# A recurrent scan wholly in 64x64 products, its transposed inverse carried through the solve, its jobs in two pairs of PSUM banks

## The chip, the cores and the metric

The kernel runs on one NeuronCore of a Trainium2 chip. The metric is the device time of one execution in microseconds. Its engines are TensorE (matrix products, PE in the rows, with the loading of weights as PEld), VectorE (DVE), ScalarE (ACT), GpSimd (POOL) and SyncE (SP, which issues the transfers here). Matrix products write to PSUM, eight banks of 2 KB in each of 128 partitions; VectorE and ScalarE copy them out.

## The reference, cut to what matters

The reference is a network of three blocks on 512 tokens of width 1024 with 256 context tokens. The second block has a recurrent scan over 16 heads of width 64, in two directions:

```python
def step(S, inp):
    w_t, k_t, v_t, kk_t, kka_t = inp[:5]
    S = (S * w_t[:, :, None, :]
         - jnp.einsum('bhij,bhj->bhi', S, kk_t)[..., None] * kka_t[:, :, None, :]
         + v_t[..., None] * k_t[:, :, None, :])
    y = jnp.einsum('bhij,bhj->bhi', S, inp[5]) if emit else None
    return S, y
```

S is a 64x64 state for each head and direction. After the scan the outputs are normalised for each head, scaled, added to a bonus term and gated. The rest (attention, pooling, the feed-forward layers, the projections) isn't touched by the change.

## The kernel before

The function `wkv` computes the scan. It takes the tokens in chunks of 64 (`CHUNK`), 12 for the 768 tokens, and replaces the steps within a chunk by matrix products and by the inverse of a triangular 64x64 matrix; only the states between chunks are passed on one after another. The heads go in eight pairs, one pair a phase `k` of `phases()`; while pair k is solved, pair k+1 is prepared and pair k-1 is finished. Three parts of the order matter.

The first is the list of *jobs* that `solve_jobs` writes out. Each job is a batch of small products into PSUM, which one engine then copies out. A pair's 12 chunks in two directions and two heads are 48 matrices, worked on in three groups g of 16. For each group M, N and I multiply the prepared keys with each other (copied by ScalarE or VectorE); K multiplies with the values. Then the inverse is built from small blocks up, in five levels (`LEVELS` is 2, 4, 8, 16, 32), three groups each, so 15 solves (`SOLVES`): Z multiplies the matrix M by the present inverse x, and VectorE keeps the part that the level adds by a predicated copy with a mask (line 2783); X multiplies that by the present inverse transposed, which gives the next inverse, and ScalarE copies it (line 2657). For X the transposed inverse is needed: U makes it by four 128x128 transposes through the identity into bank 7 (line 2445), copied by ScalarE (line 2661), anew at every level. At the last level T takes the place of X and gives the transposed inverse itself (line 2470). E, P, B and Y apply the inverse to keys and values and form what the states and the outputs need.

The second is the ring of banks. Jobs lie in banks 0 to 3, two banks wide (K's first two one), in the order of the list; a job waits until whatever lay in its banks has been copied out (`ring_free`). In the solve this gives Z one pair of banks and X the other. U has bank 7, and waits for the copy of the U before. Banks 4 and 5 serve the preparation (two alternating single banks), and bank 6 the steps from state to state and the outputs.

The third is what is woven between the jobs (`woven_stages`). After the jobs M, N, I stand the scan steps of pair k-1 (`step`, ten, 8 matmul records each) and the turns of tokens (`tok`): 14 stages of three 128x128 transposes, each copied by ScalarE. Around K and the first Z stand the low-rank products (`lora`, eight stages of one 64x128 product with 384 columns) and `ystate`; along the solve stand the sums of squares (`sums`, `yvar`), which multiply 128x128 blocks with two columns of a mask, and the spreads (`spread`, `yspread`), which hand one value back to 64 columns. Each engine runs this list in its own order; no scheduler changes it. SyncE only loads each pair's inputs and stores its result.

A 64x64 product is addressed to one of four quarters of the array, by the half of the partitions that its inputs lie in and the half that its output goes to. Z, X, M, N and I rotate over all four; K and E use only the two where rows and columns are the same half, since their output partitions are those of the input (`ps[f, ...]`).

## Time and profile before

| | us |
|---|---|
| median of three runs | 3102.48 |
| lowest and highest | 3100.88, 3104.81 |
| span of the profiled execution (slowest and only core) | 3107.0 |
| TensorE busy | 2828.0 (91%) |
| VectorE busy | 1827.1 (59%) |
| ScalarE busy | 1219.8 (39%) |

The profile gives no other time for its execution than the span, from its first to its last instruction. TensorE's busy time counts matmuls whose ends are modelled and overlap, so four products on four quarters count once; a full row doesn't mean an engine at its peak. The scan stands between about 1228 and 1900 us of the span. In the rows, `residual` and `work` are memory that the scan borrows: `residual` holds M and the inverse x (and, in the listing of the changed kernel, both inverses), `work` the tokens, the starting inverse and its transpose.

### The profile page before, as it was taken

The numbers are of one execution on the slowest core, as the hardware profiler recorded it, in microseconds if no ns is written. First come the engines' busy times: TensorE is split into PE (matmuls) and PEld (weight loads), VectorE is DVE, ScalarE is ACT, GpSimd is POOL, SyncE is SP. The second block draws the span as 40 slices with busy tenths as digits, with TensorE's granted clock in tenths as the row PEclk, the third lists the DMA queues.
The fourth block names the chain that finished last, engine by engine and source line by source line (L and its number), as shares of the span: only waits on it lengthen the run. The fifth ranks groups of instructions, "written<-read, shape, count | busy, mean of one in ns | idle before, by whom it ended". The sixth has DMA issues, their size and how long they took to land. (4 is left out here: it accounts for less than half of the span.)

```text
span 3107.0 us, 66043 instructions
## 1 busy us (share of the span) xinstructions
PE 2828.0 (91%) x28892; PEld 2454.0 (79%) x28892; DVE 1827.1 (59%) x2841; ACT 1219.8 (39%) x2024; POOL 18.9 (1%) x25
## 2 busy tenths in 40 slices
PE   4988989999997998898899988899998898889998
PEld 4977989999996887677777776688886685678887
DVE  7656775655446644666666655755567644466642
ACT  4326343222224433555555543433334324454421
POOL 0011000000000000000000000000000000000000
PEclk9999989999996999999999998899998898999999
DMA  6320223333321323100000003355531210123332
GB/s 256 121 87 23 89 94 124 127 138 126 122 80 57 114 96 128 32 24 10 25 26 26 26 13 112 120 181 178 176 111 57 61 42 8 55 75 96 101 94 83
DMA packets 89981, 272.88 MB, mean 88 GB/s; under 512 B 9441, under 2 KB 14689, under 8 KB 89569
## 3 DMA queue, kind: packets, MB, share of 16 engines
q1 hardware_dynamic: 85088, 258.17, 24.4%
q10 hardware_dynamic: 4608, 10.49, 1.0%
q8 instruction: 231, 3.78, 0.5%
q14 instruction: 54, 0.43, 0.0%
HBM read 252.11 MB, written 16.52 MB: 86 GB/s over the span
## 5 line engine op out<-in xcount | busy, mean ns | idle before, releaser
L427 DVE TENSOR_TENSOR weights_low<-raw_weights,weights_high 128x1024 fp32r<-128x1024 f32 (+3 forms) x333 | 356.5, 1072 | 704.5 <-ACT weights_high L396 703.8
L396 ACT ACTIVATE weights_high<-raw_weights 128x1024 fp32r<-128x1024 f32 (+3 forms) x333 | 310.9, 935 | 975.1 <-PE psum L223 934.2
L223 PE MATMUL psum<-mlp_in_high,weights_high 128*128 128x512 f32 (+1 forms) x1120 | 371.4, 368 | 21.5 <-DVE mlp_in_low L964 16.4
L223 PE MATMUL psum<-mlp_in_low,weights_high 128*128 128x512 f32 (+1 forms) x1120 | 369.9, 367 | 0.0
L223 PE MATMUL psum<-mlp_in_high,weights_low 128*128 128x512 f32 (+1 forms) x1120 | 369.7, 367 | 0.0
L223 PEld LDWEIGHTS psum<-mlp_in_high,weights_high 128*128 128x128 f32 x1120 | 208.7, 190 | 49.3 <-issue 17.6
L223 PE MATMUL psum<-hidden_high,weights_high 128*128 128x384 f32 (+1 forms) x768 | 229.5, 352 | 0.0
L223 PE MATMUL psum<-hidden_low,weights_high 128*128 128x384 f32 (+1 forms) x768 | 229.5, 352 | 0.0
L223 PE MATMUL psum<-hidden_high,weights_low 128*128 128x384 f32 (+1 forms) x768 | 229.4, 352 | 0.0
L223 PEld LDWEIGHTS psum<-mlp_in_low,weights_high 128*128 128x128 f32 x1120 | 209.1, 190 | 24.2
L223 PEld LDWEIGHTS psum<-mlp_in_high,weights_low 128*128 128x128 f32 x1120 | 208.8, 190 | 24.3
L2783 DVE COPY_PREDICATED wkv_z<-wkv_levels,psum 128x512 f32<-128x512 int32 x120 | 87.9, 733 | 103.6 <-PE psum L2466 101.9
L223 PEld LDWEIGHTS psum<-hidden_high,weights_low 128*128 128x128 f32 x768 | 140.5, 188 | 10.1
L223 PEld LDWEIGHTS psum<-hidden_low,weights_high 128*128 128x128 f32 x768 | 140.5, 188 | 10.0
L223 PEld LDWEIGHTS psum<-hidden_high,weights_high 128*128 128x128 f32 x768 | 140.5, 188 | 9.9
L223 PE MATMUL psum<-mixed_high,weights_high 128*128 128x384 f32 (+1 forms) x360 | 108.5, 366 | 25.4 <-DVE mixed_low L1309 11.9
L223 PE MATMUL psum<-h_high,weights_high 128*128 128x384 f32 (+2 forms) x312 | 100.7, 372 | 23.4 <-DVE h_low L964 20.2
L223 PE MATMUL psum<-mixed_low,weights_high 128*128 128x384 f32 (+1 forms) x360 | 105.6, 358 | 0.0
L223 PE MATMUL psum<-mixed_high,weights_low 128*128 128x384 f32 (+1 forms) x360 | 105.4, 358 | 0.0
L699 DVE CUSTOM_DVE_ANT_0 pool_u<-pool_u,conditions 128x1024 f32<-128x1024 f32 x80 | 97.6, 1220 | 0.8
L223 PE MATMUL psum<-h_high,weights_low 128*128 128x384 f32 (+2 forms) x312 | 97.6, 363 | 0.0
L223 PE MATMUL psum<-h_low,weights_high 128*128 128x384 f32 (+2 forms) x312 | 97.5, 362 | 0.0
(477 smaller groups left out, 5581.2 us busy)
## 6 DMA issues: line engine op xcount, KB each, us to landing
raw_weights<-in_mlp_w SPq DMA_DIRECT2D x96, 512.0 KB, 4.3
mod_space<-in_ada SPq DMA_DIRECT2D x56, 512.0 KB, 3.7
pool_u<-in_ada SPq DMA_DIRECT2D x56, 512.0 KB, 3.6
raw_weights<-in_w_up SPq DMA_DIRECT2D x44, 512.0 KB, 3.5
work<-in_ada SPq DMA_DIRECT2D x32, 512.0 KB, 4.8
raw_weights<-in_mlp_w SPq DMA_DIRECT2D x64, 256.0 KB, 2.9
raw_weights<-in_w_down SPq DMA_DIRECT2D x16, 512.0 KB, 3.5
raw_weights<-in_w_in SPq DMA_DIRECT2D x12, 512.0 KB, 4.8
```

Of the source, the lines that this page charges most:

```text
L223: last = nc.tensor.matmul(out[:, a, :] if wide else out, w[:, cols], x[:, at, t0:t1], start=first, stop=final)
L396: nc.scalar.activation(halves_of(ph, j)[0], raw_of(ph, j), ACT.Copy).then_inc(high.sem, 1)
L427: nc.vector.tensor_tensor(lo, raw_of(ph, j), hi.bitcast(F32), ALU.subtract).then_inc(split.sem, 1)
L699: ins = nc.vector.tensor_tensor_reduce(out=self.junk, in0=self.w[:, slot, :], in1=vector, scale=1.0, scalar=0.0, op0=ALU.mult, op1=ALU.add ...
L2783: last = nc.vector.copy_predicated(two(Z[:, i // GROUPS, i % GROUPS % 2, :]), level(2 + i // GROUPS), ps[:, b:b + 2, 0:4 * CHUNK])
```

## The change

The transposed inverse is no longer made anew at each level by transposes. U remains for the three starting inverses, as 16 products of 64x64 with a 64x64 identity; after that T, which multiplies the old transposed inverse by the masked product, runs at every level and not only at the last, 15 jobs in place of 3. Z's result is laid out so that T's and X's outputs fall in the partitions that the next level wants, and the masks follow this. All jobs of the list, U too, take a pair of banks, and all share two pairs, (0,1) and (2,3), in turn (`ring_slots`); bank 7 holds the bonus. K and E write to all four quarters.

In the woven stages every product is 64x64 in its weights: seven turns of tokens with 24 products each in place of 14 with three transposes, which now use banks 4 and 5 together; four lora stages of four products in place of eight of one; sums, variances, mean, spreads and bonus are split likewise. Sums, mean, variances and the outputs' spread move from bank 6 to banks 4 and 5. The two operations of VectorE that read a spread are cut along the half banks. The core of the diff:

```diff
-        jobs += [("M", g, 2, "SV" if g else "S"), ("N", g, 2, "V"), ("I", g, 2, "V")]
-    jobs += [("K", 0, 1, "S"), ("K", 1, 1, "S"), ("K", 2, 2, "S")]
-    for i in range(SOLVES + 2):
+        jobs += [("M", g, "SV" if g else "S"), ("N", g, "V"), ("I", g, "V")]
+    jobs += [("K", g, "S") for g in range(GROUPS)]
+    for i in range(SOLVES + 1):
         if i < SOLVES:
-            jobs.append(("Z", i, 2, "V"))
+            jobs.append(("Z", i, "V"))
         if i < GROUPS:
-            jobs.append(("U", i, 0, "S"))
-        if 1 <= i <= SOLVES:
-            jobs.append(("X" if i - 1 < SOLVES - GROUPS else "T", i - 1, 2, "S"))
-        if 2 <= i and i - 2 < SOLVES - GROUPS:
-            jobs.append(("U", i - 2 + GROUPS, 0, "S"))
-    jobs += [("E", g, 2, "S") for g in range(GROUPS)]
+            jobs.append(("U", i, "S"))
+        if i >= 1:
+            if i - 1 < SOLVES - GROUPS:
+                jobs.append(("X", i - 1, "S"))
+            jobs.append(("T", i - 1, "S"))
+    jobs += [("E", g, "S") for g in range(GROUPS)]
     for g in range(GROUPS):
-        jobs += [("P", g, 2, "V"), ("B", g, 2, "V")]
-    return jobs + [("Y", 0, 2, "V")]
+        jobs += [("P", g, "V"), ("B", g, "V")]
+    return jobs + [("Y", 0, "V")]
...
+def ring_slots(jobs):
+    used = {0: -2, 2: -1}
+    held, place, earlier = {}, {}, {}
+    for at, (name, i, _) in enumerate(jobs):
+        b = min((0, 2), key=lambda b: used[b])
+        place[name, i], earlier[name, i] = b, (held.get(b), False)
+        held[b], used[b] = (name, i), at
+    for job, (before, _) in earlier.items():
+        if before is None:
+            earlier[job] = held[place[job]], True
+    return place, earlier
...
-    at = {("M", 0): [("tok", 0), ("tok", 1), ("step", 1)], ("N", 0): [("tok", 2), ("tok", 3), ("step", 2)],
...
+    at = {("M", 0): [("tok", 0), ("step", 1)], ("N", 0): [("tok", 1), ("step", 2)],
...
+                def ring_free(k, name, i):
+
+                    job, again = earlier[name, i]
+                    if k or not again:
+                        pe.wait_ge(*(by_vector if job in kept_v else by_scalar)(k - again, *job))
+                    if again and place[name, i] == 6:
+                        pe.wait_ge(*prep_kept(k, 3))
+                        if k >= 1:
+                            pe.wait_ge(y_kept.sem, y_kept.base + k)
...
-                                        f = rows_of(o)
-                                        n = (d * 2 + j) * 2 + h
-                                        weights = XT[f, i, h * 4 * CHUNK:(h + 1) * 4 * CHUNK][:, by_tile_order(d, j)]
-                                        last = nc.tensor.matmul(ps[f, b, n * CHUNK:(n + 1) * CHUNK], weights,
+                                        f, to, n = rows_of(o), rows_of(j), d * 2 + h
+                                        weights = XX[f, i, 1, h * 4 * CHUNK:(h + 1) * 4 * CHUNK][:, by_tile_order(d, j)]
+                                        last = nc.tensor.matmul(ps[to, b + o, n * CHUNK:(n + 1) * CHUNK], weights,
                                                                 TOK[f, 2, own(tile_of(d, 2 * i + j), h)], start=True, stop=True)
...
+                                        f, to, c = rows_of(o), rows_of(d), (h * 2 + j) * CHUNK
+                                        last = nc.tensor.matmul(ps[to, b + o, c:c + CHUNK], X1[f, i, unit(h, d, j)], EYE[f, :],
+                                                                start=True, stop=True)
...
-                            last = nc.tensor.transpose(ps[:, 7, c], x[:, c], core.ident[:, :])
...
+                                        f, to, c = rows_of(o), rows_of(side), (h * 2 + same) * CHUNK
+                                        last = nc.tensor.matmul(ps[to, b + o, c:c + CHUNK], AA[f, g, unit(h, d, j)],
+                                                                x[f, x_columns(level - 1, h, d, j)], start=True, stop=True)
...
+                                        f, to, c = rows_of(side), rows_of(o), (h * 2 + same) * CHUNK
+                                        last = nc.tensor.matmul(ps[to, b + side, c:c + CHUNK], XX[f, g, 1, t_columns(level - 1, h, d, j, o)],
+                                                                Z[f, level, g % 2, z_columns(level, h, d, j, o)], start=True, stop=True)
...
+                                        side, over = row_side(level, d, j), row_side(level + 1, d, j)
+                                        f, to, c = rows_of(side), rows_of(over), (h * 2 + o) * CHUNK
+                                        last = nc.tensor.matmul(ps[to, b + side, c:c + CHUNK],
+                                                                Z[f, level, g % 2, z_columns(level, h, d, j, o)],
+                                                                XX[f, g, 1, t_columns(level - 1, h, d, j, o)], start=True, stop=True)
...
-                                        f, u = rows_of(o), unit(h, d, j)
-                                        n = (d * 2 + j) * P
-                                        last = nc.tensor.matmul(ps[f, b + h, n:n + P], XT[f, i, u],
-                                                                RHS[f, d, (2 * i + j) * 2 + h, :, :].rearrange("p s c -> p (s c)"),
+                                        f, to, n = rows_of(j), rows_of(o), (h * 2 + d) * P
+                                        last = nc.tensor.matmul(ps[to, b + j, n:n + P], XX[f, i, 1, t_columns(len(LEVELS) - 1, h, d, j, o)],
+                                                                RHS[f, i, o, d * 2 + h, :, :].rearrange("p s c -> p (s c)"),
                                                                 start=True, stop=True)
...
-                        for j in range(3):
-                            t = n % 2 * 3 + j
-                            if n // 2 in (1, 2, 3, 4):
-
-                                t = tile_of((n // 2 - 1) % 2, t)
-                            last = nc.tensor.transpose(ps[:, prep_bank(k, TURN + n), j * P:(j + 1) * P],
-                                                       src[:, t * P:(t + 1) * P], core.ident[:, :])
...
+                        for p in range(tiles):
+                            t = tile_of((n - 1) % 2, p) if 1 <= n <= 4 else p
+                            for o in range(2):
+                                for h in range(2):
+                                    f, to = rows_of(h), rows_of(p % 2 if 1 <= n <= 2 else o)
+                                    c = (p // 2 * 2 + o if 1 <= n <= 2 else p) * CHUNK
+                                    last = nc.tensor.matmul(ps[to, 4 + h, c:c + CHUNK], src[f, at_chunk(t, o)], EYE[f, :],
+                                                            start=True, stop=True)
...
-                        nc.tensor.matmul(ps[:, prep_bank(k, BONUS), :], core.head_sum[:, :], BON[:, :], start=True, stop=True)\
-                            .then_inc(prep_done.sem, 1)
...
+                        for h in range(2):
+                            f = rows_of(h)
+                            last = nc.tensor.matmul(ps[f, 7, :], core.ones[f, 0:HEAD], BON[f, :], start=True, stop=True)
...
-                                last = nc.tensor.matmul(ps[rows_of(h), prep_bank(q, SPREAD + n), j * P:(j + 1) * P],
-                                                        small[:, 0, 1, 2 * t + h:2 * t + h + 1].to_broadcast([P, HEAD]),
-                                                        core.ident[:, :], start=True, stop=True)
...
+                                    last = nc.tensor.matmul(ps[rows_of(h), 4 + o, t * CHUNK:(t + 1) * CHUNK],
+                                                            small[f, 0, 1, c:c + 1].to_broadcast([HEAD, HEAD]), EYE[f, :],
+                                                            start=True, stop=True)
...
-                    elif name == "T":
-                        last = act(by_tile(XT[:, i % GROUPS, :]), filled(b), ACT.Copy)
-                    elif name == "U":
-                        last = act(XT[:, i % GROUPS, :].rearrange("p (o m c) -> p m o c", o=2, c=CHUNK),
-                                   ps[:, 7, :].rearrange("p (m o c) -> p m o c", o=2, c=CHUNK), ACT.Copy)
+                        last = act(two(XX[:, i % GROUPS, 0, :]), half_pair(name, i), ACT.Copy)
+                    elif name in "TU":
+                        last = act(two(XX[:, i % GROUPS, 1, :]), half_pair(name, i), ACT.Copy)
                     else:
-                        for h in range(2):
-                            last = act(MX[:, i, h * 512:(h + 1) * 512], ps[:, b + h, :], ACT.Copy)
+                        last = act(two(MX[:, i, :]), ps[:, b:b + 2, :], ACT.Copy)
```

In the solve, TensorE's list reads as follows before, around the spreads of `X6` (L2466 is Z, L2468 X, L2445 U, L2585 and L2630 the two spreads):

```order
L2468 MATMUL psum<-wkv_z,work 64x64 x16
L2585 MATMUL psum<-constants,wkv_small 64x128 x12
L2630 MATMUL psum<-constants,wkv_small 64x128 x8
L2445 MATMUL psum<-constants,residual 128x128 x4
L2466 MATMUL psum<-residual 64x64 x16
```

And in the changed kernel at the same place (L2481 is Z, L2493 X, L2506 T, L2637 the first spread; the second now stands two solves later):

```order
L2481 MATMUL psum<-residual,work 64x64 x16
L2493 MATMUL psum<-wkv_z,residual 64x64 x16
L2637 MATMUL psum<-wkv_eye,wkv_small 64x64 x24
L2506 MATMUL psum<-residual,wkv_z 64x64 x16
L2481 MATMUL psum<-residual,work 64x64 x16
```

Four transposes of 128x128 between X and Z have become 16 products of 64x64. Each f32 product of this kind leaves two matmul records in a trace, each transpose one.

At the start of a pair, TensorE before (L2409 M and N of group 0, L2418 I, L2407 M and N of later groups, L2554 the turns, L2602 the scan steps):

```order
L2409 MATMUL psum<-wkv_exc_rho,wkv_a 64x64 x16
L2554 MATMUL psum<-constants,wkv_v 128x128 x6
L2602 MATMUL psum<-wkv_b,wkv_t 64x64 x4
L2409 MATMUL psum<-wkv_exc_rho,wkv_kd 64x64 x16
L2554 MATMUL psum<-constants,wkv_exc_rho 128x128 x6
L2602 MATMUL psum<-wkv_s,wkv_t 64x64 x4
L2418 MATMUL psum<-wkv_a,wkv_exc_rho 64x64 x16
L2554 MATMUL psum<-constants,wkv_exc_rho 128x128 x3
```

And in the changed kernel (L2436, L2445, L2434 are the same jobs, L2595 the turns, L2654 the steps):

```order
L2436 MATMUL psum<-wkv_exc_rho,wkv_a 64x64 x16
L2595 MATMUL psum<-wkv_eye,wkv_v 64x64 x24
L2654 MATMUL psum<-wkv_b,wkv_t 64x64 x4
L2436 MATMUL psum<-wkv_exc_rho,wkv_kd 64x64 x16
L2595 MATMUL psum<-wkv_eye,wkv_exc_rho 64x64 x24
L2654 MATMUL psum<-wkv_s,wkv_t 64x64 x4
L2445 MATMUL psum<-wkv_a,wkv_exc_rho 64x64 x16
L2595 MATMUL psum<-wkv_eye,wkv_exc_rho 64x64 x24
```

The places of jobs, turns and steps stay; a turn of three or six transposes has become one of 24 products.

## Rows read from the trace of the kernel before

**Rows 1.** The page: span, and TensorE's matmul row of part 1.

```profile
span 3107.0 us, 66043 instructions
PE 2828.0 (91%) x28892; PEld 2454.0 (79%) x28892; DVE 1827.1 (59%) x2841; ACT 1219.8 (39%) x2024; POOL 18.9 (1%) x25
```

**Rows 2.** Windows of one pair: sections A, B and C; columns in the first line.

```profile
core 0: us, PE busy (x) PEld busy (x) DVE busy (x) ACT busy (x) POOL busy (x), PEclk, DMA share, GB/s
1325.48:1350.47 24.99, 24.72 (x584) 19.21 (x584) 16.36 (x37) 13.93 (x30) 0.00 (x0) 1.00 0.07 19
1350.47:1388.47 38.00, 34.00 (x1089) 27.87 (x1088) 24.80 (x39) 24.51 (x45) 0.00 (x0) 1.00 0.01 3
1388.47:1405.77 17.30, 13.40 (x472) 12.21 (x463) 10.07 (x19) 3.85 (x7) 0.00 (x0) 1.00 0.27 80
```

**Rows 3.** Timeline of a solve: start, duration, engine, line, operation, count [idle before].

```profile
1375.18 0.69 PE L2466 MATMUL psum<-residual 64*64 64x64 f32 x32
1375.69 0.66 PE L2468 MATMUL psum<-wkv_z,work 64*64 64x64 f32 x32
1375.94 0.73 DVE L2783 COPY_PREDICATED wkv_z<-wkv_levels,psum 128x512 f32<-128x512 int32 x1
...
1376.28 0.66 PE L2445 MATMUL psum<-constants,residual 128*128 128x128 f32 x4
1376.40 0.60 ACT L2657 ACTIVATE residual<-psum 128x512 f32<-128x512 f32 x1 [0.53 <-PE psum L2468]
...
1376.86 0.69 PE L2466 MATMUL psum<-residual 64*64 64x64 f32 x32
```

**Rows 4.** Timeline of TensorE between two gaps marked issue, later in the solve.

```profile
1378.48 0.46 PE L2468 MATMUL psum<-wkv_z,work 64*64 64x64 f32 x16 [0.69 <-issue]
1378.88 0.66 PE L2445 MATMUL psum<-constants,residual 128*128 128x128 f32 x4
1379.46 0.69 PE L2466 MATMUL psum<-residual 64*64 64x64 f32 x32
1379.98 0.65 PE L2468 MATMUL psum<-wkv_z,work 64*64 64x64 f32 x32
1380.56 0.66 PE L2445 MATMUL psum<-constants,residual 128*128 128x128 f32 x4
1381.14 0.69 PE L2466 MATMUL psum<-residual 64*64 64x64 f32 x32
1381.65 0.29 PE L2468 MATMUL psum<-wkv_z,work 64*64 64x64 f32 x4
1382.50 0.68 PE L2468 MATMUL psum<-wkv_z,work 64*64 64x64 f32 x28 [0.55 <-issue]
```

**Rows 5.** Timeline of TensorE: three pairs of neighbouring gaps, least, median and greatest distance.

```profile
1400.85 0.45 PE L2498 MATMUL psum<-wkv_a_ga,residual 64*64 64x128 f32 x8 [0.80 <-issue]
...
1404.32 0.27 PE L2533 MATMUL psum<-wkv_gk,work 64*64 64x64 f32 x1 [0.23 <-issue]
...
1780.19 0.45 PE L2466 MATMUL psum<-residual 64*64 64x64 f32 x13 [0.20 <-issue]
...
1784.12 0.62 PE L2466 MATMUL psum<-residual 64*64 64x64 f32 x25 [0.42 <-issue]
...
1464.00 0.27 PE L2466 MATMUL psum<-residual 64*64 64x64 f32 x1 [0.86 <-issue]
...
1468.82 0.45 PE L2466 MATMUL psum<-residual 64*64 64x64 f32 x13 [1.13 <-issue]
```

**Rows 6.** The page, part 3, DMA queues: packets, MB, share of 16 engines' span.

```profile
q8 instruction: 231, 3.78, 0.5%
```

**Rows 7.** Timeline of TensorE: the bonus product, two K jobs, and the E jobs.

```profile
1340.29 1.12 PE L2560 MATMUL psum<-wkv_bonus,constants 128*128 128x512 f32 x2
...
1345.80 2.03 PE L2430 MATMUL psum<-work 64*64 64x64 f32 x64
...
1388.47 5.42 PE L2481 MATMUL psum<-residual,work 64*64 64x128 f32 x91
```

**Rows 8.** A window at the start of the first pair, columns as in group 2.

```profile
1249.00:1250.40 1.40, 1.15 (x33) 1.03 (x34) 1.36 (x3) 0.00 (x0) 0.00 (x0) 0.50 0.00 0
```

More of the change, by code:

```diff
@@ L2134, in wkv @@
     jobs = solve_jobs()
-    positions, at = [], 0
-    kept_s, kept_v, place = {}, {}, {}
+    place, earlier = ring_slots(jobs)
+    kept_s, kept_v = {}, {}
     n_s = n_v = 0
-    for name, i, width, keeper in jobs:
+    for name, i, keeper in jobs:
         if "S" in keeper:
@@ L2572, in stage @@
+                        for h in range(2):
+                            for d in range(2):
+                                f, c = rows_of(d), which * P + h * HEAD
+                                last = nc.tensor.matmul(ps[rows_of(h), b + d, 0:T0 // 2], ups[f, c:c + HEAD],
+                                                        (lora_w, lora_a)[which][f, a * T0 // 2:(a + 1) * T0 // 2], start=True, stop=True)
+                        last.then_inc(prep_done.sem, 1)
                     elif name == "sums":
@@ L2617, in stage @@
                         pe.wait_ge(y_kept.sem, y_kept.base + k)
-                        nc.tensor.matmul(ps[:, 6, :], core.head_mean[:, :], Y0[:, :], start=True, stop=True)\
-                            .then_inc(mean.sem, 1)
+                        if k < DT:
+                            pe.wait_ge(*(lora_kept(q, LORAS) if q < DT else turn_kept(k, 6)))
+                        for h in range(2):
+                            f = rows_of(h)
+                            last = nc.tensor.matmul(ps[f, 4, :], core.head_mean[f, f], Y0[f, :], start=True, stop=True)
+                        last.then_inc(mean.sem, 1)
                     elif name == "yvar":
@@ L2727, in _ @@
                 for k in phases():
[L2728 removed]
+                    for name, i, keeper in jobs:
                         if 0 <= k < DT and "S" in keeper:
@@ L3629, in wkv_masks @@
     both = [(level(1).T, level(1)), (level(1), level(1).T)]
[L3630 removed]
+    inverse = [(level(n), level(n).T) for n in LEVELS[1::2]]
+    sided = [level(n) for n in LEVELS[0::2]]
     last = [(i < j, i > j), (i <= j, i >= j)]
[L3632 to L3635 removed]
+    across = [np.concatenate((d0, d1, d0, d1), axis=1) for d0, d1 in inverse]
+    out = [np.concatenate((d0, d0, d1, d1), axis=1) for d0, d1 in both + last]
+    out = [np.concatenate([m, m], axis=0) for m in out[:len(both)]] + \
+        [np.concatenate([np.tile(sided[n // 2], 4), np.tile(sided[n // 2].T, 4)], axis=0) if n % 2 == 0
+         else np.concatenate([across[n // 2], across[n // 2]], axis=0) for n in range(len(LEVELS))] + \
+        [np.concatenate([m, m], axis=0) for m in out[len(both):]]
+    return np.stack(out, axis=1).astype(np.float32)
 def lay_out(i):
```

357 lines of the change are left out of this document (182 added, 175 removed).

## The prediction

> **What bounds the kernel now.** I read the page first, for the span and for the number of TensorE instructions [rows 1]; then the lines by tile, to find the stage that the change touches; then its windows [rows 2]; then the timeline of that stage, first for one undisturbed iteration of the solve [rows 3], then for the places where TensorE waits for nothing that the profile shows [rows 4, 5].
>
> The span is 3107.0 us [rows 1]; outside the scan nothing changes. A pair of heads costs about 80.3 us, in three sections [rows 2]: A (M, N, I, K, the turns of tokens, the scan steps) 24.99 us with 584 matmul records, B (the solve: Z, U, X, T) 38.00 us with some 1086, C (E, P, B, Y) 17.30 us with 472 in the window, 456 by the program. There are eight pairs, some 640 us together; the first lacks the scan steps, the last the preparation of a next pair.
>
> In B an undisturbed iteration takes 1.68 us: Z starts at 1375.18, X 0.51 later, U 0.59 after that, the next Z 0.58 after U [rows 3]. Thirty-two records of a 64x64 job are issued in 0.51 us, 16 ns each. But 15 iterations of 1.68 are 25 us, not 38. Part of the rest is woven work; part is gaps marked "issue". These gaps recur with a strange regularity. From 1378.48 to 1382.50 there are 16+4+32+32+4+32+4 = 124 matmul records and then 0.55 us of nothing [rows 4]. Each record has its weight load, so that is 248 instructions, and with the waits between them about 256. The page has a queue of kind "instruction" with 231 packets and 3.78 MB, 16.4 KB each [rows 6]; 2 x 28,892 TensorE instructions [rows 1] over 231 packets is 250 a packet. So a gap stands where TensorE has used up one packet of its program and the next has not come. Over the eight pairs I find 15 neighbouring gaps that are 123 to 127 records apart; their distances go from 3.47 us (1400.85 to 1404.32) over a median of 3.93 (1780.19 to 1784.12) to 4.82 (1464.00 to 1468.82) [rows 5]. A block of some 124.5 records seems not to come faster than once in 3.9 us, whatever is in it. Section B before uses 8.7 blocks in 38.0 us, 4.4 us each: it is already near that limit.
>
> The page "Runtime: NRT & Kernel Launch" of the Trainium skill, section "Instruction fetch mechanics", also has blocks of 256 instructions fetched while the current one runs, and says that crossing a block costs little and is mostly hidden, because instructions are consumed more slowly than they are fetched. The size agrees with the 124 records; the hiding does not, with gaps of 0.55 and 1.13 us [rows 4, 5].
>
> **The change part by part.** What it does to the number of TensorE records per pair is what I cost first. A 64x64 product in f32 is two records (32 for 16 products), a transpose through the 128x128 identity is one (4 for 4) [rows 3].
> - U: 15 jobs of 4 go (-60), 3 jobs of 32 come (+96). T: 3 jobs of 32 become 15 (+384).
> - In B also: key sums 12 to 48, variances 8 to 32, the two spreads 24 to 48 and 16 to 32, mean 2 to 4, the last lora 4 to 8: +36 +24 +24 +16 +2 +4. B goes from 1086 to 1612 records.
> - In A: 14 turns of 3 transposes (42) become 7 of 24 products (336), lora 12 to 24, bonus 2 to 4: 584 becomes 892. C keeps 456.
>
> The sum is 2960 against 2126, 23.8 blocks against 17.1.
>
> Section B. 1612/124.5 = 12.95 blocks. One is ready when the section begins, and I let it run at its own pace, 2.6 us; the others come at 3.93: 11.95 x 3.93 + 2.6 = 49.6 us, against 38.00: +11.6. By 3.64 a block it would be 46.1, by 4.4 it would be 55.2.
>
> Beneath that cover lies the ring. Before, Z and X each had a pair of banks and U bank 7; now Z, X and T share two pairs, and each job waits until the one two before it is copied out. X to its copy's end is 0.71 + 0.60 us (1375.69, 1376.40), Z's 0.76 + 0.73 (1375.18, 1375.94) [rows 3]; with 0.15 to restart TensorE (my choice, from copies that a U followed) these are 1.46 and 1.64. Three jobs over two pairs of banks: (1.64 + 1.46 + 1.46)/2 = 2.28 us an iteration, against 1.68. But 96 records at 124.5 in 3.93 us are 3.03 us an iteration. So the ring's wait costs nothing as long as instructions come this slowly; without that cover it is +0.6 an iteration.
>
> Section A. Up to the bonus there are 688 records, 5.5 blocks: 4.5 x 3.93 + 2.6 = 20.4 us, against 14.8 before (1325.48 to 1340.29 [rows 2, 7]). Behind it come K, lora and the states' product, 204 records; large products, 10.2 us before, which the stream doesn't hold up. K loses something: its 64 records take 2.03 us, 32 ns each, as they use two quarters of the array, and now use four at 16 ns [rows 7]; 96 records save 1.5 us of TensorE, of which I take 0.7, because the lora copies on ScalarE are one behind another there. 9.5 us. A: 29.9, +4.9.
>
> Section C. E's first 91 records take 5.42 us, 60 ns each, on two quarters [rows 7]. On four, about 30 ns, a job takes 0.95 us, and the copies of twice 512 columns (2 x 0.60 at most, by X's copy [rows 3]) decide: the second E is copied 0.95 + 0.25 + 2.4 = 3.6 us after the first began, and P, which takes its banks, starts there instead of 5.2 us behind. I take -1.8. C has 3.7 blocks, 14.4 us at 3.93, below the 15.5 left, so the saving stands, with little to spare.
>
> All else I cost at nothing: ScalarE copies as many solve jobs as before, half as many turns at twice the width; VectorE's work is the same but for operations cut in two. The turns hold banks 4 and 5 together now, so each waits for the copy of the one before, some 0.9 us for 768 columns by X's 0.60 for 512; an M, N or I job and a scan step lie between two turns, 0.65 to 1.1 us of TensorE, so it is 0 to 0.3 us each, 0 to 2 a pair. I take 0, since it lies beneath the stream's wait. ScalarE is busy 24.5 of B's 38 us and VectorE 24.8 [rows 2]. Spreads and sums take less of TensorE as 64x64 products (48 records at 16 ns are 0.8 us), but that time is given back to waiting for the next block.
>
> Per pair: +11.6 +4.9 -1.8 = +14.7 us. The first pair has 2748 records, the last 2832; I count the eight as 7.8 full ones: +115 us. Against its own span that is 3222. The span stands 4.5 us above the median of 3102.48 of the runs, so I predict 3217.
>
> "TensorEngine Tiling (Array Packing)" of the Trainium skill, section "Key Properties", says that a change of tiling mode drains TensorE. By it this change gains, since all modes but 64x64 leave the scan. The trace shows X to U 0.59 and Z to X 0.51 us apart [rows 3], 0.08 us a change. Some 60 changes a pair would be 5 us, and by that alone the sum would be 3063.
>
> **The rivals.**
> 1. Faster: the instruction stream isn't what limits. If the gaps were something else (a record lost, a semaphore), the mode changes, K, E and the cheaper spreads and sums would show. A gives back 1.8 us; B pays 0.6 x 6 for the ring in its undisturbed iterations and gives back 4.8 (my estimate: spreads 1.3, sums 1.0, mode changes 1.0, gaps 1.5); C gives back 1.8. That is -4.8 a pair, 3065 us. It decides at one point: A+B+C, by the sums above, is 16.5 L + 30.2, and this is 80.3 where L, the time of a block, is 3.04 us. All 15 measured are above (the least 3.47 [rows 5]). For it speaks only that records at 16 ns and no gap would allow 2.0 us a block. The Trainium skill's two rules above, fetching that is hidden and a mode change that drains, would both lead here.
> 2. Slower, but by the ring: blocks come in some 3.0 us when asked for early, and the two pairs of banks set 2.28 us an iteration: +8.9 in B less 4.8 for A, C and the spreads, +4 a pair, 3135 us. Against it stand the 3.03 us an iteration by [rows 5].
> 3. The clock falls too. In B 96 records of 16 ns in 3.0 us leave TensorE half idle. At the lower level (granted 0.50, 1.2 GHz) 33 records were busy 1.15 us [rows 8], against 0.69 for 32 at the full level. Before, all three sections ran at 1.00 [rows 2] with a gap of 1.1 us in the middle. Three jobs would then take 3.0 us an iteration, as long as the stream, and every wait would be 0.45 longer: some +4 a pair more, 3250 us.
>
> **How the numbers follow.** Forecast (the stream of instructions sets the pace) 0.75; rival 1 0.07; rival 2 0.10; rival 3 0.08. The forecast's own range is 3.64 to 4.2 us a block, 3180 to 3250. To leave out no more than 2 in 10 I go from 3135, which takes in rival 2, to 3270. What can be told from no change is 0.2%, 6 us. Slower: 0.75 + 0.10 + 0.08 = 0.93, less 0.03 for a rival 2 that comes out even: 0.90. Within 0.2%: 0.03. Faster: 0.07.
>
> **What would show it.** The packets of the instruction queue rise from 231 to about 283 (6550 more records in eight pairs, 13,100 instructions). B's window grows to about 50 us with TensorE's busy share falling, gaps marked "issue" at nearly every 124th record, 3.6 to 4.2 us apart, and few in C. The first E to P shrinks from 5.2 to about 3.5 us. VectorE's wait for Z grows though Z is no longer. Wrong would be: gaps further apart than 4.8 us or none while B still grows (then the ring, with TensorE waiting for ScalarE's copies of X and T), a granted clock below 0.95 in B, or a pair under 80 us.

## The result, and the profile after

The changed kernel takes 3197.72 us (3185.94 to 3200.68, four runs) against 3103.64 of the kernel before on the same chip: ratio 1.0291, 95% interval 1.0269 to 1.0314. That is 94 us more by the medians and 90 by the ratio; 115 were forecast, and 3217 us. The page after answers to [rows 1] and [rows 6]:

```profile
span 3193.2 us, 78968 instructions
PE 2787.4 (87%) x35564; PEld 2433.5 (76%) x35564; DVE 1826.9 (57%) x2849; ACT 1215.5 (38%) x1928; POOL 18.9 (1%) x25
...
q8 instruction: 282, 4.62, 0.6%
```

TensorE has 6672 matmul records more (eight times 834) and is busy 41 us less, in a span that is 86 us longer: it waits more. VectorE and ScalarE do the same work as before. The instruction queue brought 282 packets in place of 231.

The windows of pair 1, answering to [rows 2], sections A, B and C:

```profile
1332.26:1360.73 28.47, 22.73 (x893) 18.80 (x896) 14.47 (x35) 13.38 (x21) 0.00 (x0) 1.00 0.07 18
1360.73:1409.38 48.65, 33.81 (x1617) 28.87 (x1613) 26.54 (x42) 24.86 (x45) 0.00 (x0) 0.96 0.02 4
1409.38:1426.13 16.75, 11.53 (x471) 9.80 (x462) 10.22 (x19) 3.56 (x4) 0.00 (x0) 1.00 0.26 84
```

The means over pairs 1 to 6, which I use from here on, are 25.13, 38.16 and 17.06 us before and 28.82, 47.35 and 15.38 after: +3.7, +9.2, -1.7, together +11.2 us a pair. Times 7.8 that is 87 us, and the span grew by 86.2. In B TensorE's work is as long as it was for half as many records again, and TensorE's busy share falls from 90% (34.45 of 38.16) to 73% (34.51 of 47.35).

The timeline of TensorE late in a solve, for [rows 3] to [rows 5] (L2481 is Z, L2493 X, L2506 T, L2518 E):

```profile
1676.33 0.62 PE L2481 MATMUL psum<-residual,work 64*64 64x64 f32 x27 [0.48 <-issue]
...
1677.83 0.69 PE L2506 MATMUL psum<-residual,wkv_z 64*64 64x64 f32 x32 [0.35 <-DVE wkv_z L2842]
1678.35 0.65 PE L2481 MATMUL psum<-residual,work 64*64 64x64 f32 x32
1679.24 0.33 PE L2493 MATMUL psum<-wkv_z,residual 64*64 64x64 f32 x3 [0.25 <-ACT residual L2721]
1679.94 0.63 PE L2493 MATMUL psum<-wkv_z,residual 64*64 64x64 f32 x27 [0.37 <-issue]
...
1683.57 0.63 PE L2481 MATMUL psum<-residual,work 64*64 64x64 f32 x28 [0.37 <-issue]
...
1687.18 2.48 PE L2518 MATMUL psum<-residual 64*64 64x128 f32 x65 [0.47 <-issue]
```

Four gaps stand 3.61, 3.63 and 3.61 us apart, and between the last two there are 28+1+3+31+32+31 = 126 records by the rows left out. Over the eight pairs there are some 108 gaps of at least 0.15 us marked issue, 76.8 us in all, against 33 and 18.3 us before; over 70 of them follow the one before by one block, at a median of 3.65 us. Between the gaps waits for VectorE and ScalarE stand, and by the marks they are the larger part: in B a pair's waits for ScalarE's copies are 6.2 us (1.7 before), those marked issue 4.5 (1.5 before), those for VectorE 1.8 (0.5 before). So the marks alone don't say whether the stream or the ring of banks sets the pace; the experiments do.

The traces also hold the packets of the instruction queue one by one, each 16,384 bytes. Every gap marked issue in the scan, 33 before and over 100 after, ends 1.20 to 1.60 us after such a packet has been moved; 1676.33 to 1687.18, for example, has packets that end at 1678.54, 1682.36 and 1685.66 us, and TensorE resumes at 1679.94, 1683.57 and 1687.18. Of the waits put down to ScalarE only 12 of 138 end that long after a packet, of those to VectorE 5 of 64. So a gap marked issue ends with the arrival of instructions.

K and E, for [rows 7] (L2456 is K, L2538 P), and the start of the first pair, for [rows 8]:

```profile
1357.81 0.64 PE L2456 MATMUL psum<-work,residual 64*64 64x64 f32 x32
...
1775.26 2.03 PE L2518 MATMUL psum<-residual 64*64 64x128 f32 x64
1777.48 1.10 PE L2518 MATMUL psum<-residual 64*64 64x128 f32 x32 [0.19 <-ACT residual L2723]
1778.44 0.59 PE L2538 MATMUL psum<-wkv_a_ga,residual 64*64 64x64 f32 x24
```

```profile
1246.69:1248.09 1.40, 1.40 (x52) 1.40 (x56) 1.36 (x3) 0.20 (x1) 0.00 (x0) 0.50 0.00 0
```

E to P takes 3.18 us here, where no gap falls into it, and 4.0 to 4.6 us in the pairs where one does; it was about 5.2. The first pair begins at the granted clock of 0.50 (1.2 GHz), as before.

### The profile page after: what moved, and what is told of

It is laid out like the page before. It is cut to its first block and busy times, and to the rows that moved or that the text cites. A ratio compares the mean times of both kernels' runs of the same rounds, so it can differ in the third digit from the quotient of the medians.

```text
span 3193.2 us, 78968 instructions
## 1 busy us (share of the span) xinstructions
PE 2787.4 (87%) x35564; PEld 2433.5 (76%) x35564; DVE 1826.9 (57%) x2849; ACT 1215.5 (38%) x1928; POOL 18.9 (1%) x25
## 5 line engine op out<-in xcount | busy, mean ns | idle before, releaser
L223 PEld LDWEIGHTS psum<-hidden_high,weights_high 128*128 128x128 f32 x768 | 140.5, 188 | 10.1
L2721 ACT ACTIVATE residual<-psum 128x512 f32<-128x512 f32 x144 | 85.6, 595 | 80.9 <-PE psum L2506 68.3
L2506 PE MATMUL psum<-residual,wkv_z 64*64 64x64 f32 x3840 | 95.3, 231 | 22.0 <-issue 11.5
L2493 PE MATMUL psum<-wkv_z,residual 64*64 64x64 f32 x3072 | 75.5, 233 | 39.0 <-ACT residual L2721 29.8
```

Source lines behind the costliest of these rows:

```text
L223: last = nc.tensor.matmul(out[:, a, :] if wide else out, w[:, cols], x[:, at, t0:t1], start=first, stop=final)
L2493: last = nc.tensor.matmul(ps[to, b + side, c:c + CHUNK], XX[f, g, 1, t_columns(level - 1, h, d, j, o)], Z[f, level, g % 2, z_columns(level ...
L2506: last = nc.tensor.matmul(ps[to, b + side, c:c + CHUNK], Z[f, level, g % 2, z_columns(level, h, d, j, o)], XX[f, g, 1, t_columns(level - 1 ...
L2721: last = act(two(XX[:, i % GROUPS, 1, :]), half_pair(name, i), ACT.Copy)
```

## The experiments

Ratios are to the kernel before, in runs on the same chip. The kernel before takes 3109.89 us beside the first four, so by its ratio the changed kernel would take about 3200 us there. Two theories were set against each other: the stream (a block of some 125 records comes no faster than once in 3.65 us) and the ring (three solve jobs wait for each other's copies in two pairs of banks); a third is the sheer work of TensorE.

**t_turned: T below the last level by transposes, still in the ring.** From the changed kernel:

```diff
-            jobs.append(("T", i - 1, "S"))
+            jobs.append(("X" if i - 1 < SOLVES - GROUPS else "T", i - 1, "S"))
+        if 2 <= i and i - 2 < SOLVES - GROUPS:
+            jobs.append(("T", i - 2, "S"))
...
+                            pe.wait_ge(*by_scalar(k, "X", i))
+                            for side in range(2):
+                                for h in range(2):
+                                    c = side * 256 + h * P
+                                    out = ps[:, b + side, h * P:(h + 1) * P]
+                                    last = nc.tensor.transpose(out, XX[:, g, 0, c:c + P], core.ident[:, :])
```

> In the changed kernel the transposed inverse of the levels below the last is made again by four 128x128 transposes of X's result, in the same ring of two pairs of banks; all else stays, 64x64 products included. That is 28 matmul records less in each of 12 jobs a pair, 1276 in place of 1612 in the solve. If the stream of instructions sets the pace (3.65 us a block of 125 records, the median of the changed kernel's profile), the solve falls from 47.6 to about 38.5 us a pair and the kernel to about 3125 us. If the ring of banks sets it, the solve stays: 3190 to 3200 us. If TensorE's own work sets it, 12 jobs at 0.59 us take the place of 12 at 0.51: 3195 to 3205 us.

Measured: 3158.33 us, ratio 1.0156 (1.0134 to 1.0178). B falls from 47.35 to 42.71 us, A and C rise by 0.5 and 0.7. The sign is the stream's, the size lies between the two: 42 us of the 75 came.

**tok_turned: five of the seven turns of tokens by transposes.**

```diff
+                            if not 1 <= n <= 2:
+                                a, m = (p % 2, p // 2) if n > 2 and n < 5 else (p // 3, p % 3)
+                                last = nc.tensor.transpose(ps[:, 4 + a, m * P:(m + 1) * P], src[:, t * P:(t + 1) * P], core.ident[:, :])
+                                continue
```

> In the changed kernel five of the seven turns of tokens are made by six 128x128 transposes each again, 210 records less in section A of a pair; the solve is untouched. Stream of instructions: A falls from 28.5 by up to 1.7 blocks, 6 us, less what the changes of tile mode give; I expect 4 us a pair, the kernel near 3165 us. If the drains at changes of mode were what counts, ten of them come back a pair at some 0.1 us each: 3198 to 3210 us.

Measured: 3185.37 us, ratio 1.0243 (1.0223 to 1.0263). A falls from 28.82 to 26.32 us, but B rises from 47.35 to 48.77. The 210 records fewer a pair are 1.7 blocks, 6.2 us, of which A gave 2.5 and B took 1.4 back. The sign is again the stream's, at under half the size.

**wide_z: Z streams its operand twice, 128 columns in place of 64, with the same instructions and copies.**

```diff
-                                        last = nc.tensor.matmul(ps[to, b + o, c:c + CHUNK], AA[f, g, unit(h, d, j)],
-                                                                x[f, x_columns(level - 1, h, d, j)], start=True, stop=True)
+                                        out = ps[to, b + o, :].rearrange("p (a l) -> p a l", a=2)[:, :, c:c + CHUNK]
+                                        last = nc.tensor.matmul(out, AA[f, g, unit(h, d, j)],
+                                                                x[f, x_columns(level - 1, h, d, j)].unsqueeze(1).to_broadcast([HEAD, 2, CHUNK]),
+                                                                start=True, stop=True)
```

> In the changed kernel every product of the Z jobs streams its operand twice, the second copy into the unused half of the bank: 128 columns in place of 64, the same number of instructions, copies and waits. By the M and N jobs this makes a Z job some 0.45 us longer on TensorE, 6.7 us a pair. Stream of instructions: that is hidden while the next block is awaited, under 1 us a pair, 3195 to 3205 us. TensorE's work: +54 us, 3250 us. Ring of banks: Z's copy comes 0.45 us later, half of it in each iteration, +3.4 us a pair, 3225 us.

Measured: 3211.4 us, ratio 1.0328 (1.0305 to 1.0351), some 11 us above the changed kernel: more than the 3205 that the stream allowed, less than the ring's 3225, and far from the 3250 of TensorE's work. Its B by six windows, first and sum (the changed kernel's sum is 284.12 with PE 207.08):

```profile
1364.86:1413.96 49.10, 38.66 (x1617) 33.77 (x1612) 26.39 (x42) 24.94 (x45) 0.00 (x0) 0.97 0.02 4
...
sum 294.84, PE 235.36 PEld 204.64 DVE 158.87 ACT 149.83 POOL 0.00; mean PE 39.23 PEld 34.11 DVE 26.48 ACT 24.97 POOL 0.00
```

TensorE is busy 4.7 us a pair more in B, by the columns 480 records of 16 ns, 7.7 us, and B is 1.8 us longer, where under 1 was expected by the stream and 3.4 by the ring. TensorE's work isn't what holds section B, but a longer Z isn't wholly hidden either.

**both_turned: both of the first two edits.** Its diff is theirs together.

> Both edits before this one together, the levels' transposes and the five turns of tokens by 128x128 transposes: 2414 records a pair in place of 2960 (2126 in the kernel before). Stream of instructions: the two gains add, 3125 and 3165 from 3198 give about 3090 us, at which the stream is no longer short everywhere and the ring's waits begin to show; I expect 3095 us. Ring: 3190 us or more.

Measured: 3130.78 us, ratio 1.0065 (1.0044 to 1.0087), 36 us above the 3095 expected by the stream and well below the ring's 3190. The gaps fall to 35 with 24.3 us, nearly as few as before, so most of the stream's pressure is gone; yet B stays at 42.49 us. Here the ring can be seen (L2493 X, L2481 Z, L2506 T; L2732 is ScalarE's copy of T, L2730 of X):

```profile
1703.40 0.69 PE L2481 MATMUL psum<-residual,work 64*64 64x64 f32 x32
1703.51 0.60 ACT L2732 ACTIVATE residual<-psum 128x512 f32<-128x512 f32 x1 [1.07 <-PE psum L2506]
1704.16 0.69 PE L2493 MATMUL psum<-wkv_z,residual 64*64 64x64 f32 x32
...
1704.95 0.66 PE L2506 MATMUL psum<-constants,residual 128*128 128x128 f32 x4
...
1705.57 0.69 PE L2481 MATMUL psum<-residual,work 64*64 64x64 f32 x32
```

X begins 0.76 us after Z though Z's 32 records are issued in 0.51: T's copy frees its banks at 1704.11. An iteration is 2.17 us, against 1.68 [rows 3]. Where ScalarE has something else before that copy, X waits longer:

```profile
1701.07 0.69 PE L2493 MATMUL psum<-wkv_z,residual 64*64 64x64 f32 x32 [1.04 <-ACT residual L2732]
```

**out_of_ring: both_turned with those transposes in bank 7, outside the ring; the bonus moves to bank 4.**

```diff
+        if name == "T" and i < SOLVES - GROUPS:
+            place[name, i], earlier[name, i] = 7, (held.get(7), False)
+            held[7] = (name, i)
+            continue
         b = min((0, 2), key=lambda b: used[b])
```

> This is the kernel with levels' transposes and turns by transposes (3130.78 us, 0.65% above the kernel before), with the transposes of the levels put back into bank 7, outside the ring of two bank pairs; the three first U and the last three T stay in the ring. TensorE issues the same records in the same order. If what is left in section B (42.5 us against 38.2 in the kernel before, with 35 gaps in place of 108) is the ring, where each Z waits for the copy of the X or T two jobs before, B falls to about 38.5 us and the time by 4 us x 7.8 = 31 us to about 3100 us, a ratio of 0.997. If it is the stream of instructions, nothing changes: 3130 us, ratio 1.0065. If it is work of TensorE (the spreads, sums and lora as many small products), nothing changes either, and B stays at 42.5 us with few waits for ScalarE or VectorE.

Measured: 3106.96 us, ratio 1.0009 (0.9998 to 1.0021). B falls by 3.4 us, from 42.49 to 39.07. Six windows of B in both_turned, and in out_of_ring, by their sums:

```profile
sum 254.96, PE 208.63 PEld 166.43 DVE 161.16 ACT 149.68 POOL 0.00; mean PE 34.77 PEld 27.74 DVE 26.86 ACT 24.95 POOL 0.00
```

```profile
sum 234.42, PE 192.86 PEld 160.04 DVE 161.28 ACT 146.90 POOL 0.00; mean PE 32.14 PEld 26.67 DVE 26.88 ACT 24.48 POOL 0.00
```

In B TensorE's waits for ScalarE go from 4.4 us a pair to 1.3, and gaps marked issue come back: 77 with 53.7 us in place of 35 with 24.3. An iteration without a gap is 1.67 us again:

```profile
1708.27 0.70 PE L2485 MATMUL psum<-residual,work 64*64 64x64 f32 x32
...
1709.94 0.70 PE L2485 MATMUL psum<-residual,work 64*64 64x64 f32 x32
```

So the ring is real, and behind it the stream is met once more. Its size is less sure than the 3.4 us: the granted clock differed. In both_turned three pairs ran B at 1.00 and took 40.84, 40.95 and 41.65 us, and one ran at 0.85 and took 45.51; in out_of_ring four ran at 1.00, at a mean of 39.18. By the pairs at 1.00 alone the ring is worth 2.0 us. The ratio gives 17 us, 2.2 a pair, the spans 24.7 (3131.5 and 3106.8); expected were 31. The waits that the profile marks don't fall in sum (6.5 and 6.9 us a pair); the gain stands in TensorE's busy time, which takes in the start of each wait, as 32 records are issued in 0.51 us and count as busy for 0.69.

**fewest: out_of_ring with low-rank products, sums, variances and spreads in 128 rows again.** Of its diff, the sums:

```diff
-                            for o in range(2):
-                                for h in range(2):
-                                    f = rows_of(h)
-                                    last = nc.tensor.matmul(ps[rows_of(o), 4 + h, t:t + 1], SQ[f, at_chunk(t, o)], core.ones[f, 0:1],
-                                                            start=True, stop=True)
+                            last = nc.tensor.matmul(ps[:, 4, t:t + tiles + 1:tiles], SQ[:, t * P:(t + 1) * P],
+                                                    core.head_sum[:, 0:P:HEAD], start=True, stop=True)
```

> The kernel of out_of_ring with the low-rank products, sums, variances and spreads again as products of 128 rows, some 116 records a pair fewer (2298 against 2414; the kernel before has 2126). What stays of the change: Z, X and E laid out for four quarters, the turns with three transposes each in banks 4 and 5, and K, P and E on four quarters. By the stream: 116 records are 0.93 blocks of 124.5; where blocks limit, 3.65 us a pair, but few gaps are left (24 us in all), so I expect 1 to 2 us a pair, 8 to 15 us: 3085 to 3092 us, ratio 0.992 to 0.995. By the ring as the only cause: the same as out_of_ring within 3 us. By the mode change: eight lora products a pair and the spreads of 64x128 change mode again, 0.08 us each, some 30 a pair, +2.4 us a pair: slower than out_of_ring by 10 to 20 us.

Measured: 3102.11 us, ratio 0.9985 (0.9976 to 0.9994). B falls to 37.5 us, but A rises from 25.8 to 26.4: a gain of 7 us by ratios, under the 8 to 15 expected (3085 to 3092 us). In section A it shows two waits, of which the kernel before has only the second, at 0.26 us in place of 0.38:

```profile
1507.46 0.38 PE L2666 MATMUL psum<-wkv_s,wkv_t 64*64 64x64 f32 x5 [1.04 <-DVE wkv_s L2960]
...
1508.76 0.92 PE L2629 MATMUL psum<-lora_input,wkv_ups 64*128 64x384 f32 x4 [0.38 <-DVE wkv_bonus_value L2886]
```

**leaner: fewest with a change against each of those two waits, the bonus in bank 7 and the low-rank stage ahead of the ninth step.**

```diff
-          ("I", 2): [("bonus", 0), ("step", 9)],
-          ("K", 0): [("lora", 0), ("step", 10)], ("K", 1): [("lora", 1), ("square", 0), ("decay", 0)],
+          ("I", 2): [("bonus", 0), ("lora", 0), ("step", 9)],
+          ("K", 0): [("step", 10)], ("K", 1): [("lora", 1), ("square", 0), ("decay", 0)],
...
-                            last = nc.tensor.matmul(ps[f, 4, :], core.ones[f, 0:HEAD], BON[f, :], start=True, stop=True)
+                            last = nc.tensor.matmul(ps[f, 7, :], core.ones[f, 0:HEAD], BON[f, :], start=True, stop=True)
```

> The kernel of fewest (3102.11 us, 0.15% under the kernel before), with its new waits in section A taken away: the bonus is back in bank 7 (the transposes of the levels, which have that bank since, are done by then), so the first low-rank stage no longer waits for VectorE to use the bonus (0.38 us idle in fewest's third pair), and that stage moves ahead of the ninth scan step, which waited 1.04 us for the state copied before it. The records are the same, 2298 a pair. In fewest section A is 26.4 us against 25.1 before, with 2.2 us a pair of waits for VectorE against 1.1. If these two waits are what A lost, A falls by 1.0 to 1.4 us a pair, 8 to 11 us in all: 3091 to 3095 us, ratio 0.995 to 0.996. If A is held by the stream or by the double-width turns of tokens, which wait for the copy of the one before: no change within 3 us.

Measured: 3083.11 us, ratio 0.9934 (0.9920 to 0.9948): it is faster than both kernels, and by more than the 0.995 to 0.996 expected. A falls by 1.27 us to 25.11, as the two waits said in sum, but not by them alone. The bonus's wait is gone; the state's 1.04 us is now 0.20 before the ninth step and 0.68 before the tenth; and a wait of 0.96 us of the next low-rank stage for ScalarE (decay) is gone too. B and C fall by 0.85 and 0.67, which was not expected. In part that is the choice of runs: the profile is of the fastest of leaner's five runs (3077.46 us), and fewest's is of the second slowest of twelve (3104.23). The spans differ by 26.8 us, the ratios by 16, and A's 1.27 us a pair is 10. Its B:

```profile
1347.31:1384.11 36.80, 34.13 (x1175) 28.53 (x1173) 26.09 (x40) 24.50 (x45) 0.00 (x0) 0.95 0.02 4
...
sum 220.02, PE 198.61 PEld 165.75 DVE 155.62 ACT 146.89 POOL 0.00; mean PE 33.10 PEld 27.63 DVE 25.94 ACT 24.48 POOL 0.00
```

**burst: the kernel before with 1024 independent products at the start of the scan.** Nobody reads what they write.

```diff
+                for n in range(1024):
+                    f, to = rows_of(n % 2), rows_of(n // 2 % 2)
+                    nc.tensor.matmul(ps[to, 6 + n % 2, 0:CHUNK], core.ident[f, 0:CHUNK], core.ident[f, 0:CHUNK],
+                                     start=True, stop=True)
```

> The kernel before with 1024 independent 64x64 products of the identity (2048 matmul records, 4096 instructions, 16.4 blocks) at the start of TensorE's program of the scan, into two banks that nothing else holds there, with no wait between them; their output is read by nobody. They measure the block period by itself. By the stream: the gaps stand 124 to 128 records apart, and a block takes 3.5 to 3.9 us whatever it holds: 16.4 x 3.65 = 60 us more, ratio 1.019; TensorE is busy 2.0 us of each 3.7. By work alone: 16 ns a record at the full clock, 33 us more, or up to 66 us at the lower granted clock with no gaps marked issue. If the period depends on waits and semaphores of the scan, not on the number of instructions: no gaps, 33 us.

Measured: 3166.45 us, ratio 1.0204 (1.0187 to 1.0221), 63 us. TensorE's timeline, the whole burst but for rows that repeat:

```profile
1227.06 3.95 PE L2637 MATMUL psum<-constants 64*64 64x64 f32 x252 [1.29 <-PEq L349]
1235.10 3.69 PE L2637 MATMUL psum<-constants 64*64 64x64 f32 x128 [4.09 <-issue]
1239.37 2.79 PE L2637 MATMUL psum<-constants 64*64 64x64 f32 x128 [0.58 <-issue]
1243.10 2.10 PE L2637 MATMUL psum<-constants 64*64 64x64 f32 x128 [0.94 <-issue]
1246.57 2.10 PE L2637 MATMUL psum<-constants 64*64 64x64 f32 x128 [1.37 <-issue]
1250.31 2.10 PE L2637 MATMUL psum<-constants 64*64 64x64 f32 x128 [1.65 <-issue]
...
1287.45 0.33 PE L2637 MATMUL psum<-constants 64*64 64x64 f32 x4 [1.38 <-issue]
```

No semaphore, no copy, no bank is waited for, and still TensorE stops after every 128 records exactly. From 1239.37 to 1287.45 there are 13 blocks, 3.70 us each (3.45 to 4.01), of which 2.10 are work (2.79 in the first). Two blocks less four records are issued in one piece at the start, the first after a long idle time.

The packets of the instruction queue show what a period is made of. After TensorE resumes behind a gap, the next packet starts 1.05 to 1.76 us later, takes 0.88 to 1.36 us, and TensorE resumes again 1.19 to 1.55 us after its end: the block resumed at 1243.10, for example, is followed by a packet from 1244.23 to 1245.35, and the next block by TensorE at 1246.57. So in burst the packet of a block moves only when the block before it has begun, and the sum of these three is the 3.70 us.

**burst_wide: the same burst, each product with 128 columns.**

```diff
-                    nc.tensor.matmul(ps[to, 6 + n % 2, 0:CHUNK], core.ident[f, 0:CHUNK], core.ident[f, 0:CHUNK],
+                    nc.tensor.matmul(ps[to, 6 + n % 2, 0:P], core.ident[f, 0:CHUNK], core.ident[f, 0:P],
```

> The burst of 1024 independent products at the start of the scan once more, as many instructions in the same order, but each product streams 128 columns in place of 64, so TensorE has twice the work: 32 ns a record where 64 columns took 16 (the kernel before's K jobs on two quarters, 64 records in 2.03 us, are the nearest row). The burst with 64 columns took 60.6 us up to the first low-rank product, 3.70 us a block of 128 records, of which TensorE was busy 2.10. By the stream: a block of 128 records now has 4.1 us of work, longer than the 3.7 us that the next one takes to come, so the gaps marked issue go (below 0.3 us each) and the burst takes 16 x 4.1 = 66 us, only 5 us more than with half the work; ratio about 1.022. By a cost that goes with the work: twice 60.6, 121 us, ratio 1.039. By a fixed pause of 1.6 us after every 128 records, whatever they hold: 16 x (4.1 + 1.6) = 91 us, ratio 1.029.

Measured: 3162.14 us, ratio 1.0175 (1.0161 to 1.0190).

```profile
1237.11 51.72 PE L2637 MATMUL psum<-constants 64*64 64x128 f32 x1796 [2.77 <-issue]
1288.76 1.56 PE L2569 MATMUL psum<-lora_input,wkv_ups 64*128 64x384 f32 x8
```

```profile
1239.37:1283.98 44.61, 44.60 (x1604) 44.10 (x1600) 0.00 (x0) 0.00 (x0) 0.00 (x0) 0.99 0.02 4
```

Twice the work ends 1.05 us later than half of it (1288.76, against 1287.71 in burst), and the gaps are gone: 1604 records in 44.61 us are 27.8 ns each, 3.56 us for 128 (4.1 were expected), just about as long as a block takes to come. A cost that goes with the work (121 us) and a pause after every block (91 us) both fall. By the ratios burst costs 63 us and burst_wide 54, on two chips, though its own products take 1 us more; that difference is not explained.

## Why the prediction was right, and where its sizes were off

The forecast, that the stream of TensorE's instructions sets the pace, held; its reasons held in the runs as follows.

- **The block.** Packets 282 for the 283 forecast. The period was taken as 3.93 us from 15 pairs of gaps before [rows 5]; under steady demand it is 3.65 (over 70 pairs after) and 3.70 (burst). A gap before was often seen beside other waits, and those lengthened its distance. This is the term that was mis-sized. With 3.65 the prediction's own sums give 11.95 x 3.65 + 2.6 = 46.2 for B (47.35 measured) and 19.0 for the first part of A (19.72 in pair 1, from 1332.26 to the bonus at 1351.98), +10.1 us a pair and +79 us in all; measured were +11.2 a pair. So the true price lies between, nearer to this one, and the rest is other waits beside the stream's, which a sum of blocks leaves out.
- **Section B**, +11.6 forecast, +9.2 measured. That the rule is about the number of instructions and not about their work is shown by the two bursts and borne out by wide_z.
- **Section A**, +4.9 forecast, +3.7 measured: 19.7 for 20.4 up to the bonus, 8.75 for 9.5 behind it in pair 1. The last part was to gain 0.7 from K, and gained 1.4: 32 records of K are issued in 0.47 us (1357.81 to 1358.28), as many took 1.0 [rows 7].
- **Section C**, -1.8 forecast, -1.7 measured, and E to P is 3.18 us for the forecast 3.5 where no gap falls into it. That C has few gaps was wrong: 1.95 us a pair marked issue stand in it, against 0.78 before. The saving came all the same.
- **The ring at nothing beneath the stream.** This step is only half right. It held for the total: 12.95 blocks of 3.65 us are 47.3, and B is 47.35, so the 6.2 us of waits for ScalarE lie beneath the blocks. But "without that cover it is +0.6 an iteration" has measured 0.49 (2.17 against 1.68), and the cover is thin: B stays near 42.5 us in this ring in both t_turned and both_turned (42.71 and 42.49 us, with 69 gaps and with 35), and falls to 39.07 out of it. That both_turned took 3131 us, near the 3135 of the ring's rival, is chance: the rival had B at +8.9 us, and both_turned's is at +4.3. The expectation of t_turned, 3125, failed on this: it let B fall to the stream's next price and forgot the ring that lies near 42.5. What the ring adds while the stream is at its full length was not tried by itself.
- **The clock.** The rival that it falls was given 3250 us. The granted clock in B was 0.96, 0.96, 0.89, 0.93, 0.96 and 0.96 in the six pairs, against 1.00, 0.96, 1.00, 0.95, 0.96 and 1.00 before. So the mark that I had set, below 0.95, was met in two of six. Its price isn't visible in the changed kernel, where the pair at 0.89 took 47.31 us in B and one at 0.96 took 48.65; once the stream is relieved it is (45.51 us at 0.85 against 41.15 at 1.00 in both_turned). A clock of 0.943 in the mean is 11% of the time at the lower level, 5.4 us a pair; against 1.7 us before, and at half of the speed, this is 1.9 us a pair at most, if nothing covered it.
- **The faster rival** needed a block below 3.04 us, and none of the distances after was below 3.40. Its mode changes don't outweigh the records: both_turned, out_of_ring, fewest and leaner brought transposes and 128-row products back among the 64x64 ones, and each was faster than the changed kernel.

"Runtime: NRT & Kernel Launch" of the Trainium skill, section "Instruction fetch mechanics", gives blocks of 256 instructions, and burst agrees to the record (128, each with its weight load). That crossing one is mostly hidden holds in burst_wide, where a block's work lasts 3.56 us, and not in burst, where it lasts 2.10.

What the change gives is what leaner keeps: E and K on four quarters, the layout of Z and X for it, seven turns of double width. These were not tried one by one. In leaner's profile, of its fastest run, with them and with the count taken back from 2960 to 2298 records a pair (2126 before), A is 25.1, B 36.7, C 15.2, together 77.0 us against 80.35.

## What to carry to other kernels

Count instructions of TensorE as a resource of its own: where small products follow each other densely, 256 instructions (128 matmuls with their loads) cost about 3.65 us here, with 2.1 us of work in them as with 3.6, so a matmul below some 28 ns is paid as 28 ns. Four 128x128 transposes that do the work of sixteen 64x64 products (4 records for 32) are then worth more than a better use of the array. To tell such a gap from others, set it beside the packets of the instruction queue. When such a limit is taken away, look for the next one at once, as here the ring of banks near 42.5 us, and price an experiment by the nearer of the two. Before windows of two profiles are compared, compare their runs and their clocks: a profile of a fast run against one of a slow run gave 26.8 us here where the ratios gave 16.

## What was not expected of the hardware

- With the stream as the limit, twice the columns are almost free: 2048 records took 60.6 us with 64 columns and 61.6 with 128.
- TensorE issued 252 records, two blocks less four, without a gap after a long idle time (the first row of burst), and then had nothing for 4.09 us. The packet that ended this wait started only at 1232.89 us, though TensorE had run out at 1231.01; in this gap the transfers stand at 0.98 of their share, and whether they held the packet up is open.
- One execution's scan can be slower than another's without a change. The scan behind the burst is the kernel before, instruction for instruction, and still its pairs take 81.6 us behind burst and 80.5 behind burst_wide, against 80.35, with gaps marked issue of 25.3, 22.7 and 18.6 us. Where the borders of blocks fall doesn't explain it: both bursts have the same number of instructions. But burst's profile is of the slowest of its four runs (3177.47 us, the others 3163.51 to 3166.47), and 1.25 us in eight pairs is about those 11 us. A difference of some 0.3% between two single profiles of such a kernel thus needs no cause in the program.
